# Attention in halves of the array: values held still, head pairs mixed together, weights divided before they are turned

## What is computed

```python
s = jnp.einsum('bhqd,bhkd->bhqk', qb, kh) + Fb[..., None] - F[:, :, None, :]   # fox
s = jnp.where(kpos[None, :] <= qpos[:, None], s, -jnp.inf)
p = jax.nn.softmax(s, axis=-1)
return jnp.einsum('bhqk,bhkd->bhqd', p, vh)
...
y_a = y_a * jax.nn.silu(z_a)      # mla, and dsa with z_b; fox has no gate
```

## Time and profile before

| | us |
|---|---|
| median of 3 runs | 1195.56 (1195.43 to 1196.46) |
| profiled execution | 1202.39 |
| its span, first to last instruction | 1200.6 |
| PE busy in the span | 1150.1 |
| DVE, ACT, POOL busy | 579.9, 444.2, 244.6 |
| `mix` products, L1283 | 480 instructions |

### The profile page before, as it was taken

How to read it: one execution, slowest core, us unless ns; L and a number is a source line. 1 busy time by engine, 2 the same in 40 slices (tenths; PEclk the granted TensorE clock), 3 DMA queues, 4 the chain that set the end, 5 groups by cost and what they waited for, 6 DMA issues and landing times.

```text
span 1200.6 us, 14262 instructions
## 1 busy us (share of the span) xinstructions
PE 1150.1 (96%) x5524; PEld 896.2 (75%) x5524; DVE 579.9 (48%) x1049; ACT 444.2 (37%) x755; POOL 244.6 (20%) x140
## 2 busy tenths in 40 slices
PE   7799899999999999999999999998799999999995
PEld 5597766677788888888888755777787777788884
DVE  5744352435554442344444468866455333214544
ACT  6624334434523221133234545343334344313332
POOL 0631111113101100001113223312221222331101
PEclk9899799999999999999999999999899999999998
DMA  7032110111232232223233212222212221232221
GB/s 278 19 106 70 35 36 31 41 53 56 103 97 97 88 123 88 88 89 100 93 106 94 69 68 83 67 73 79 68 54 71 71 70 62 70 106 88 93 101 71
DMA packets 29892, 97.74 MB, mean 81 GB/s; under 512 B 3488, under 2 KB 4192, under 8 KB 29824
## 3 DMA queue, kind: packets, MB, share of 16 engines
q1 hardware_dynamic: 29824, 96.82, 24.3%
HBM read 94.38 MB, written 4.72 MB: 83 GB/s over the span
## 4 chain that ended last, share of the span: by engine, by line
PE 85%; DVE 8%; ACT 3%; DMA 2%; issue 2%; DVEq 0%; SPq 0%; ACTq 0%; POOL 0%; POOLq 0%
PE bank L1157 22%; PE bank L1159 21%; PE bank L1158 21%; PE bank L1283 4%; DMA WS<-wall 2%; PE bank L1276 2%; PE bank L1254 2%; PE bank L1264 2%; PE bank L1169 2%; PE bank L1170 1%; PE bank L1171 1%; PE bank L1260 1%; DVE score L1756 1%; DVE m L1765 1%; DVE WL L1542 1%
## 5 line engine op out<-in xcount | busy, mean ns | idle before, releaser
L1157 PE MATMUL bank<-HH,WH 128*128 128x512 f32 x808 | 331.0, 410 | 16.7 <-DVE WL L1542 8.2
L1159 PE MATMUL bank<-HH,WL 128*128 128x512 f32 x808 | 318.2, 394 | 0.0
L1158 PE MATMUL bank<-HL,WH 128*128 128x512 f32 x808 | 317.3, 393 | 0.0
L1836 POOL TENSOR_TENSOR WL<-WS,WH 128x1024 fp32r<-128x1024 f32 x60 | 144.0, 2400 | 458.4 <-ACT WH L1326 457.9
L1157 PEld LDWEIGHTS bank<-HH,WH 128*128 128x128 f32 x808 | 153.9, 190 | 61.1 <-issue 14.3
L1326 ACT ACTIVATE WH<-WS 128x1024 fp32r<-128x1024 f32 x164 | 170.5, 1048 | 75.1 <-PE bank L1159 42.8
L1159 PEld LDWEIGHTS bank<-HH,WL 128*128 128x128 f32 x808 | 153.1, 189 | 33.3
L1158 PEld LDWEIGHTS bank<-HL,WH 128*128 128x128 f32 x808 | 153.8, 190 | 28.9 <-issue 0.7
L1542 DVE TENSOR_TENSOR WL<-WS,WH 128x1024 fp32r<-128x1024 f32 x104 | 137.6, 1329 | 37.9 <-ACT WH L1326 37.9
L1882 POOL TENSOR_TENSOR fa<-fa,fg 128x512 f32<-128x512 f32 x22 | 28.4, 1291 | 275.1 <-DVE fa L1718 275.1
L1159 PE MATMUL bank<-GH,WL 128*128 128x512 f32 x176 | 69.5, 395 | 0.0
(11 more groups left out here) (313 smaller groups left out, 1797.4 us busy)
## 6 DMA issues: line engine op xcount, KB each, us to landing
WS<-wall SPq DMA_DIRECT2D x164, 512.0 KB, 3.5
scratch<-scratch SPq DMA_DIRECT2D x8, 317.5 KB
X<-xT SPq DMA_DIRECT2D x8, 256.0 KB, 6.2
b_t<-scratch SPq DMA_DIRECT2D x8, 256.0 KB, 3.8
outT<-X SPq DMA_DIRECT2D x5, 256.0 KB, 2.4
outT<-o_x SPq DMA_DIRECT2D x3, 256.0 KB, 2.0
icnt<-cph SPq DMA_DIRECT2D x1, 512.0 KB, 6.3
RT<-cf SPq DMA_DIRECT2D x1, 256.0 KB, 6.7
```

The lines of the kernel that those rows point to most:

```text
L1157: e.matmul(b[:, :], wh, xh[:, at_k, :], start=k == 0, stop=False)
L1158: e.matmul(b[:, :], wh, xl[:, at_k, :], start=False, stop=False)
L1159: m = e.matmul(b[:, :], wl, xh[:, at_k, :], start=False, stop=k == n - 1)
L1836: e.tensor_tensor(WL[:, u % NW, :], WS[:, u % NST, :], f32(WH[:, u % NW, :]), ALU.subtract).then_inc(*tick(w_low_g, u))
```

## The change

- `turned_at`, `strided`: a buffer `PT` of 2560 columns holds the turned weights of a whole pair. A key block's stretch of queries lies in one piece there: `[key block kb, queries 128*kb to 512]` for each head. There is one such buffer; `PTb`, `PTc`, `f_y` and `b_y` are gone.
- A new step `share` stands ahead of `turn`: DVE takes the reciprocal and multiplies `p` itself by it, in place, 128 to 512 columns. PE's `turn` now waits for `share` where it waited for the exponential.
- ACT copies a turned bank into `PT` by 128-column blocks.
- `mix` is done once per pair: for each key block and each head, the 64 value columns are stationary and 512 - 128*kb columns of `PT` move; head 0 goes to partitions 0 to 63 of the bank, head 1 to 64 to 127. The result has features on partitions already.
- `turn_y` and its step are gone; `take_y` works from the bank. For fox ACT rounds straight from the bank.
- Buffers are moved: `g_qe`, `g_kh`, `RQ`, `RK` and two of `a_half`.

```diff
+def turned_at(hl, kb):
+    return 128 + 640 * kb if hl == 0 else 1920 - 768 * kb
...
+            def step_share():
+                s = to_share.pop(0)
+                do("share", **{n: s[n] for n in ("u", "i", "p", "st")})
+                st_ring.give(s["st_i"], share(s["u"]))
+                to_b.append(s)
...
                         if to_d:
                             step_d()
+                        if to_share:
+                            step_share()
                         n, b, free = s_ring.take()
...
-                        to_b.append(s)
+                        to_share.append(s)
                         yield
-                        if len(to_b) > 1:
+                        if to_c:
+                            step_c()
+                        if to_b:
                             step_b()
-                        if len(to_c) > 1:
-                            step_c()
                         yield
...
                 elif kind == "turn":
-                    q.wait_ge(exps(s["u"]), s["free"])
-                    for kb in range(s["i"] + 1):
-                        cs = slice(kb * 128, kb * 128 + 128)
-                        m = e.transpose(s["b"][:, cs], s["p"][:, cs], ident[:, :])
+                    i = s["i"]
+                    q.wait_ge(share(s["u"]), s["free"])
+                    for kb in range(i + 1):
+                        at_b = (kb if s["hl"] == 0 else i - kb) * 128
+                        m = e.transpose(s["b"][:, at_b:at_b + 128], s["p"][:, kb * 128:kb * 128 + 128], ident[:, :])
...
-                    for kb in range(s["i"] + 1):
-                        m = e.matmul(s["b"][:, 0:64], s["pt"][:, kb * 128:kb * 128 + 128],
-                                     v[:, kb, hd * 64:hd * 64 + 64], start=kb == 0, stop=kb == s["i"])
+                    for kb in range(4):
+                        for hl in range(2):
+                            at_pt, hd = turned_at(hl, kb), 2 * p + hl
+                            m = e.matmul(b[64 * hl:64 * hl + 64, 128 * kb:512], v[:, kb, hd * 64:hd * 64 + 64],
+                                         s["pt"][:, at_pt + 128 * kb:at_pt + 512], start=kb == 0, stop=kb == 3)
...
-                elif kind == "turn_y":
-                    q.wait_ge(y_part(s["u"]), s["free"])
-                    for i in range(4):
-                        m = e.transpose(s["b"][:, i * 128:i * 128 + 128], s["yt"][:, i, :], ident[:, :])
-                    m.then_inc(*yturned.tick(s["u"]))
...
-                elif kind == "mix":
-                    st, u, i, hl = s["st"], s["u"], s["i"], s["hl"]
+                elif kind == "share":
+                    st, u, n = s["st"], s["u"], 128 * (s["i"] + 1)
                     q.wait_ge(exps(u))
                     e.reciprocal(st[:, 2:3], st[:, 1:2]).then_inc(*inverse.tick(u))
-                    q.wait_ge(mixed(u), inverse(u), s["free_yt"])
-                    e.tensor_scalar(s["yt"][:, i, 64 * hl:64 * hl + 64], s["b"][:, 0:64], st[:, 2:3], None,
-                                    ALU.mult).then_inc(*y_part.tick(u))
+                    q.wait_ge(inverse(u))
+                    e.tensor_scalar(s["p"][:, 0:n], s["p"][:, 0:n], st[:, 2:3], None, ALU.mult).then_inc(
+                        *share.tick(u))
```

More of the change, by code:

```diff
@@ L224, in build @@
         negs = [sub(f"neg{j}", [128, T], BF16, 19 + j) for j in range(3)]
-        PTb = [sub(f"PTb{i}", [128, T], F32, 72 + 2 * i) for i in range(2)]
+        PT = sub("PT", [128, 2560], F32, 84)
         g_S = sub("g_S", [128, 8, 128], F32, 76)
@@ L552, in build, with attention @@
         st_ring = Ring([small[:, 4 * i:4 * i + 4] for i in range(8)])
-        def attention(pairs, p_ring, pt_ring, yt_ring):
-            to_b, to_c, to_d = [], [], []
+        def attention(pairs, p_ring, pt_ring):
+            to_share, to_b, to_c, to_d = [], [], [], []
+            def step_share():
[3 more added lines that the diff above has]
+                to_b.append(s)
             def step_b():
                 s = to_b.pop(0)
+                if s["hl"] == 0 and s["i"] == 0:
+                    s["pair"]["pt"] = pt_ring.take()
                 i, b, free = t_ring.take()
-                j, pt, free_pt = pt_ring.take()
-                s["pt"], s["pt_i"] = pt, j
-                do("turn", u=s["u"], i=s["i"], p=s["p"], pt=pt, free_pt=free_pt, b=b, free=free)
+                _, pt, free_pt = s["pair"]["pt"]
+                do("turn", b=b, free=free, pt=pt, free_pt=free_pt, **{n: s[n] for n in ("u", "a", "hl", "i", "p")})
                 p_ring.give(s["p_i"], turned(s["u"]))
                 t_ring.give(i, moved(s["u"]))
-                to_c.append(s)
+                if s["hl"] == 1 and s["i"] == 3:
+                    to_c.append(s)
             def step_c():
@@ L569, in step_c @@
                 i, b, free = y_ring.take()
[L570 to L575, removed]
+                pt_i, pt, _ = s["pair"]["pt"]
+                do("mix", b=b, free=free, pt=pt, **{n: s[n] for n in ("u", "a", "p_no")})
+                pt_ring.give(pt_i, mixed(s["u"]))
+                to_d.append(dict(s, y_i=i, y=b))
             def step_d():
                 s = to_d.pop(0)
[L579 to L585, removed]
+                if s["a"] == "fox":
+                    do("take_y", t1=None, free1=None, **{n: s[n] for n in ("u", "a", "p_no", "y", "z")})
+                    y_ring.give(s["y_i"], low((s["to"], s["to_n"])))
+                else:
+                    j, t1, free1 = tmp_ring.take()
+                    do("take_y", t1=t1, free1=free1, **{n: s[n] for n in ("u", "a", "p_no", "y", "z")})
+                    y_ring.give(s["y_i"], gated_v(s["u"]))
+                    tmp_ring.give(j, low((s["to"], s["to_n"])))
                     s["z_ring"].give(s["z_i"], gated_v(s["u"]))
@@ L1686, in vector_program @@
                     p, t1 = s["p_no"], s["t1"]
-                    to_h, to_l = {"fox": (MH, ML), "mla": (YAH, YAL), "dsa": (YBH, YBL)}[s["a"]]
-                    key = {"fox": ("mix", 4 + p), "mla": ("ya", p), "dsa": ("yb", p)}[s["a"]]
-                    if s["a"] != "fox":
-                        q.wait_ge(yturned(s["u"]), silu(f"{'za' if s['a'] == 'mla' else 'zb'}{p}"), s["free1"])
-                        e.tensor_tensor(t1[:, :], s["b"][:, :], s["z"][:, :], ALU.mult).then_inc(*gated_v.tick(s["u"]))
@@ L1692, in vector_program @@
-                    q.wait_ge(hi(key))
-                    e.tensor_tensor(to_l[:, key[1], :], t1[:, :], f32(to_h[:, key[1], :]), ALU.subtract).then_inc(
-                        *low.tick(key))
+                    if s["a"] == "fox":
+                        q.wait_ge(hi(("mix", 4 + p)))
+                        e.tensor_tensor(ML[:, 4 + p, :], s["y"][:, :], f32(MH[:, 4 + p, :]), ALU.subtract).then_inc(
+                            *low.tick(("mix", 4 + p)))
+                    else:
+                        to_h, to_l, key = (YAH, YAL, ("ya", p)) if s["a"] == "mla" else (YBH, YBL, ("yb", p))
+                        q.wait_ge(mixed(s["u"]), silu(f"{'za' if s['a'] == 'mla' else 'zb'}{p}"), s["free1"])
+                        e.tensor_tensor(t1[:, :], s["y"][:, :], s["z"][:, :], ALU.mult).then_inc(*gated_v.tick(s["u"]))
+                        q.wait_ge(hi(key))
+                        e.tensor_tensor(to_l[:, p, :], t1[:, :], f32(to_h[:, p, :]), ALU.subtract).then_inc(
+                            *low.tick(key))
```

72 lines of the change are left out of this document (39 added, 33 removed).

## The result

The changed kernel takes 1210.34 us in the median (1205.68 to 1223.16), against 1195.49 before: a ratio of 1.0131, 95% interval 1.0083 to 1.0179. It is slower. 1173 was forecast, with 0.03 for slower, and the time lies far outside 1164 to 1186. The profiled execution took 1210.39 us with a span of 1208.6, against a span of 1200.6 before.

The account below looks back on a forecast made before the run. PE was taken to bound the kernel, except the DMA queue from 760.7 to 846.9 us. PE work 35.2 us less, minus 8.3 lost there and 4.5 of stalls, takes 22.4 off 1195.6: 1173 us, range 1164 to 1186.

Parts of the forecast that it names:

- The new mix: PE's mix per pair: two heads' halves overlap, 2.4 us per pair, 28.6 us added for 12.
- Rival 1: New mix's halves take turns on PE: 4.5 us a pair, 1194.5 us, or about 1199 with bare weight loads; chance 0.08.
- The removed mixes: Small mixes behind PE's turns: n instructions times 0.112 us plus 0.05 each, 2.44 us a head, 4.88 a pair.
- PE's balance: PE work over 12 pairs: 63.8 us removed less 28.6 added, 35.2 us less.
- The copies' stretch: mla, 760.7 to 846.9 us: the DMA queue sets the pace, so 8.3 us of saved PE work is lost.
- the shortfalls inside: Units in the copies' stretch with too little slack for the share: 6.8 us, hidden under PE's longer wait.
- The share's stalls: PE's turns waiting for the division on DVE: 4.5 us in all, with 3 and 8 as ends.
- the slack of each unit: Time from sum to turn, less the removed mix: below 0.7 us in 6 units outside the copies' stretch, 3.1 us short.
- rival 3: PE's clock falls again in fox beside gla's chain, losing 5 to 10 us: 1178 to 1183 us; chance 0.07.
- The share's own price: DVE's product 0.22 to 0.42 us; with reciprocal and handing over, a share costs 0.5 to 0.7 us.
- Rival 2: POOL's locks or DVE's order put 2.5 us between exponential and turn: 1194 us; chance 0.07, at 1181 to 1194.
- The last test of the prediction: From the copies' end to 1036 us, 189 us should shrink by 15 less 2 to 4, else the forecast is wrong.

Follow-up runs that it names:

- halves_apart: Changed kernel without the division, the new mix's four matmuls of the first head before the second's instead of alternating: 1190.44 us, ratio to before 0.9940.
- no_division: Changed kernel without reciprocal and product on DVE, the turn waiting for the exponential alone, weights undivided: 1176.26 us, ratio to before 0.9835.
- act_scale: Changed kernel with the division's product on ACT, the reciprocal staying on DVE: 1220.59 us, ratio to before 1.0176.
- before_share: Kernel before with the division ahead of the turn on DVE alone, small mixes and output turn kept: 1232.61 us, ratio 1.0297.

## Why the prediction was wrong, step by step

- **The new mix: right.** 2.4 us per pair were forecast; it is 2.31 to the first transpose behind it, and 2.36 as what it adds to that turn's block (2.39 with, 0.03 without). The halves overlap. Rival 1 was false as put; its price with the halves in turn, 4.5 us, is 3.86 in halves_apart.
- **The removed mixes: mis-sized by 5 us.** The step "n instructions times 0.112 us and 0.05 more" came from one timeline. Over all blocks at full clock, turn and mix before take 0.36, 0.69, 1.02 and 0.92 us for mixes of 2, 4, 6 and 8, and the same turns alone in the changed kernel 0.14, 0.25, 0.36 and 0.03. The mixes are 0.22, 0.44, 0.67 and 0.89: 2.22 us a head, not 2.44. The 0.05 of its own that the prediction gave each mix doesn't exist. PE's balance is 58.7 - 28.3 = 30.4 us, not 35.2. In the table the rest falls by 29.0 from before to no_division, and with the copies out of the way the two kernels differ by 25.7 us (1192.96 to 1167.30).
- **The copies' stretch: right.** 8.3 us were to be lost there. Without the division 7.3 were: the wait at the end grew by 4.8 us (9.96 to 14.80) and the shorter ones ahead of it by 2.5. The measured prices give the same, 5 x 2.22 + 2 x 0.44 - 2 x 2.36 = 7.3, and from the first copy's issue to the end of the wait it is 86.2 us before and 86.1 in no_division. In the changed kernel the waits for shares ahead of it had taken its place, as the prediction had said for the shortfalls inside; they were larger than the landing's delay, so this wait vanished and was not "9 to 12 us".
- **The share's stalls: this step failed.** It gave 4.5 us, with 3 and 8 as ends; the division costs 34 us. Three things went wrong in it.
  First, "DVE is 44% busy from 847 on, so its load is no matter". A busy share says nothing on a queue that runs in order. In the 7.4 us at 936 DVE did 2.5 us of work, and the share still came late, since what stood ahead of it waited for PE, ACT and POOL in turn.
  Second, the slack of each unit was set against the share's length (0.5 to 0.7 us), which counted only 6 units short. It had to be set against the place of the share in DVE's list: everything that stands between the previous maximum and the share, with what each of these waits for. 25.9 of 37.1 us come from that.
  Third, PE's clock: 11.5 us more are lost to it than in no_division, 9.7 of them in the second attention, where each of the six stretches at the lower level begins within 3 us of a wait of 1.4 to 3.2 us for a share. The prediction had the clock as rival 3 alone, for fox, at 5 to 10 us, and allowed 2 us in its range. That the scattered waits bring it down fits the kernels in the table, but the number of waits alone doesn't give the loss.
  The stall term was also taken low by its own terms: 3.1, 0.8 and 0.5 to 3 us add up to 4.4 to 6.9, of which 4.5 was entered.
  The share's own price was near: 0.29 to 0.49 us against 0.22 to 0.42. POOL stretched 11 shares by 14.3 us in all, more than the 0.5 to 3 us, but act_scale shows that this alone didn't set the time.
- **Rival 2 named the mechanism**, "POOL's locks or DVE's order", with a chance of 0.07 and 1194 us at most, reached at 2.5 us of delay in every unit. The trace has 28 units with 0.25 to 3.3 us of wait, and the clock on top. Its argument against, that the share would have to meet POOL each time, weighed the lock and left out the order.
- **Two slips in rival 1, without effect on the forecast.** A mix of 5.3 us would give 1202 us by the prediction's own terms, not 1199, since 2.5 us would then be lost in the copies' stretch, and the kernel would be slower from 4.6 us on. And 2 x 1280 columns are twice what a pair's mixes stream before (20 products of 64 columns), not 4 times.
- **The last test of the prediction was sound:** from the end of the copies to the last turn it was 181.4 us before (846.89 to 1028.28) and should have shrunk. It is 195.8 us now (841.35 to 1037.18).

With each part measured alone the sum closes: 1195.5, less 20.5 for the mix (no_division), plus 35.8 for the division (before_share), gives 1210.8; 1210.3 was measured.

## What to carry to other kernels

When a step moves onto the path between two engines, cost its place in the queue, not its length: list what stands ahead of it there and what each of those waits for. A low busy share is no cover. A fix by distance (one more buffer, the consumer one unit later) was worth 28 us here and one by order 9.5, where the product on an engine free of the lock gave nothing; try distance first. And before a difference between two profiles is put down to an edit, look whether it lies in a stage that the edit left alone, as much of the clock's did here.

## What the runs showed of the hardware

- Matmuls to the two column halves ran beside one another only as neighbours in the queue: 16 instructions of 128*64 took 2.31 us alternating and 3.86 us head by head, 40% less.
- A DVE product of 128 columns within SBUF beside a POOL split of 2.39 us took 1.98 us instead of 0.29; a subtraction of two SBUF operands took 2.48 instead of 0.69. The same product on ACT had one length for each size (0.39 to 0.72 us).
- PE's clock is a term of its own. Over these kernels 7 to 35 us were lost to work at the lower of its two levels, 1.2 GHz. Part of it is luck: behind the same wait of PE in fox (2.3 us) the lower level lasts 3.4 us in seven profiles and 17.1 us in five, and behind a second such wait (2.2 to 2.4 us), 40 to 50 us later, 3.4 to 17.1 us in all but one. Four runs of the changed kernel lie between 1205.7 us at a mean clock of 0.981 and 1223.2 at 0.963. The other part goes with the waits: about two dozen of up to 3.3 us (7.2 in act_scale) in the second attention cost 10 to 13 us of clock, a single one of 10 to 15 us cost 1.6 to 2.9. What decides how long the level lasts stays open.
